# Attention scores from rounded high and low parts, with query heads paired by their key head's half of the rows

## What is computed

```python
def swiglu(h, wg, wu, wd):
    return (jax.nn.silu(h @ wg) * (h @ wu)) @ wd

def dense_block_attention(q, k, v, kc, vc):
    ...
    g = hq // hk
    qb = q.reshape(bsz, nb, GA_BLOCK, hk, g, d).transpose(1, 0, 2, 3, 4, 5)
    def one_block(qi):
        s_lat = jnp.einsum('bqhgd,bkhd->bhgqk', qi, k).astype(jnp.float32) * scale
        s_ctx = jnp.einsum('bqhgd,bkhd->bhgqk', qi, kc).astype(jnp.float32) * scale
        p_lat, p_ctx = joint_softmax([s_lat, s_ctx])
        return (jnp.einsum('bhgqk,bkhd->bqhgd', p_lat.astype(v.dtype), v)
                + jnp.einsum('bhgqk,bkhd->bqhgd', p_ctx.astype(vc.dtype), vc))
```

## Time and profile before

| | us |
|---|---|
| median of three runs | 2144.75 (2143.36 to 2147.09) |
| the profiled execution, its own time | 2144.07 |
| its span | 2142.3 |
| PE busy | 2104.7 (98%) |
| PEld busy | 1776.8 (83%) |
| DVE busy | 1390.7 (65%) |
| ACT busy | 1017.3 (47%) |
| POOL busy | 570.9 (27%) |
| granted TensorE clock, mean | 0.996 of full speed |

### The profile page before, as it was taken

The page is one execution under the profiler, slowest core; times in us unless marked ns, Lnnn a source line. Parts: engine busy times, 40 slices in busy tenths (PEclk is TensorE's granted clock), DMA queues, the critical chain, the costliest instruction groups (busy, mean ns, idle before and its releaser), DMA issues.

```text
span 2142.3 us, 31623 instructions
## 1 busy us (share of the span) xinstructions
PE 2104.7 (98%) x11813; PEld 1776.8 (83%) x11813; DVE 1390.7 (65%) x2104; ACT 1017.3 (47%) x1593; POOL 570.9 (27%) x615
## 2 busy tenths in 40 slices
PE   7999999999999999999999999999999999999998
PEld 4888888988766778988888898888889888898997
DVE  4767776865676456865665685545557869776555
ACT  4544545554555543553444453222345557645444
POOL 1556554402010036343343320000013201251000
PEclk9999999999999999999999999999999999999999
DMA  9577775723333354755555465545546455676664
GB/s 311 159 212 202 185 216 168 194 80 93 100 111 91 98 167 134 207 153 160 164 161 170 141 178 157 155 138 158 152 127 165 119 134 149 170 198 179 183 182 137
DMA packets 471963, 340.61 MB, mean 159 GB/s; under 512 B 13226, under 2 KB 437654, under 8 KB 471686
## 3 DMA queue, kind: packets, MB, share of 16 engines
q1 hardware_dynamic: 441312, 238.06, 38.8%
q0 software_dynamic: 29056, 96.35, 16.1%
q10 hardware_dynamic: 1446, 4.20, 0.5%
HBM read 326.98 MB, written 12.36 MB: 158 GB/s over the span
## 4 chain that ended last, share of the span: by engine, by line
PE 92%; DVE 4%; issue 2%; ACT 1%; DMA 1%; POOL 0%; SPq 0%; DVEq 0%; ACTq 0%; POOLq 0%
PE bank L837 20%; PE bank L838 20%; PE bank L842 20%; PE bank L905 4%; PE bank L915 4%; PE bank L906 4%; PE bank L989 2%; PE bank L990 2%; PE bank L995 2%; DVE w_lo L806 1%; PE bank L1347 1%; PE bank L1323 1%; PE bank L1333 1%; PE bank L1113 1%; PE bank L1112 1%
## 5 line engine op out<-in xcount | busy, mean ns | idle before, releaser
L806 DVE TENSOR_TENSOR w_lo<-raw,w_hi 128x1024 fp32r<-128x1024 f32 (+1 forms) x442 | 570.3, 1292 | 549.1 <-PE bank L842 336.5
L796 ACT ACTIVATE w_hi<-raw 128x1024 fp32r<-128x1024 f32 (+1 forms) x442 | 461.6, 1045 | 604.9 <-PE bank L838 288.1
L837 PE MATMUL bank<-h_hi,w_hi 128*128 128x512 f32 (+1 forms) x1728 | 597.3, 358 | 2.1 <-DVE X L2049 1.5
L838 PE MATMUL bank<-h_lo,w_hi 128*128 128x512 f32 (+1 forms) x1728 | 592.0, 355 | 0.0
L837 PEld LDWEIGHTS bank<-h_hi,w_hi 128*128 128x128 f32 x1728 | 326.5, 189 | 50.1 <-issue 1.9
L842 PE MATMUL bank<-h_hi,w_lo 128*128 128x512 f32 (+1 forms) x1728 | 367.1, 355 | 0.0
L838 PEld LDWEIGHTS bank<-h_lo,w_hi 128*128 128x128 f32 x1728 | 326.7, 189 | 46.4 <-issue 1.0
L842 PEld LDWEIGHTS bank<-h_hi,w_lo 128*128 128x128 f32 x1728 | 291.5, 189 | 45.5
L837 PE MATMUL bank<-inner_hi,w_hi 128*128 128x256 f32 (+1 forms) x654 | 204.2, 334 | 0.0
L838 PE MATMUL bank<-inner_lo,w_hi 128*128 128x256 f32 (+1 forms) x654 | 203.7, 333 | 0.0
L2485 POOL DMA_DIRECT2D wm<-in_w_mod_dram x128 | 92.6, 724 | 327.3 <-DVE bank L2020 274.9
(11 more groups left out here) (300 smaller groups left out, 3224.4 us busy)
## 6 DMA issues: line engine op xcount, KB each, us to landing
wm<-in_w_mod_dram POOLq DMA_DIRECT2D x128, 512.0 KB, 4.4
raw<-in_w_in_dram SPq DMA_DIRECT2D x108, 512.0 KB, 4.0
raw<-in_ffn_w_down_dram SPq DMA_DIRECT2D x94, 512.0 KB, 4.1
raw<-in_ffn_w_gate_dram SPq DMA_DIRECT2D x88, 512.0 KB, 4.5
raw<-in_ffn_w_up_dram SPq DMA_DIRECT2D x88, 512.0 KB, 3.9
raw<-in_w_out_dram SPq DMA_DIRECT2D x24, 512.0 KB, 4.0
raw<-in_ffn_w_down_dram SPq DMA_DIRECT2D x24, 384.0 KB, 4.0
raw<-in_w_branch_dram SPq DMA_DIRECT2D x16, 512.0 KB, 4.6
```

Source lines behind the costliest of these rows:

```text
L796: act.activation(w_hi[w_slot[n]][:, 0:unit.rows, :], raw[unit.slot][:, 0:unit.rows, :], ACT.Copy).then_inc(hi_made, 1)
L806: dve.tensor_tensor(w_lo[w_slot[n]][:, 0:unit.rows, :], raw[unit.slot][:, 0:unit.rows, :], w_hi[w_slot[n]][:, 0:unit.rows, :].bitcast(F32) ...
L837: pe.matmul(psum, w_hi[s][:, k, :], hi, start=(k == 0), stop=False)
L838: mm = pe.matmul(psum, w_hi[s][:, k, :], lo, start=False, stop=False)
```

## The change

Scores are computed in three passes of fp32r: q_hi by k_hi, q_lo by k_hi, q_hi by k_lo. Each pass issues the matmul of one row half and then of the other, so that the two banks' matmuls alternate. The parts come from here:

- `q_parts`, two buffers in turn: ACT rounds the task's 128 queries (`round_q`), DVE subtracts (`split_q`). Those of tasks 0 and 1 stand ahead of the turns, those of task t+2 at the end of turn t on DVE and after `exponents(t)` on ACT. `q_parts` lies in the place of `dt_t`, whose last reader is the DMA of the cumulative sums, so ACT first waits for that (`cum_stored`).
- Keys AK and CK get their parts by a new step "keys" at positions 12 and 13 of the projection, BK and BK+1 in turns 1 and 2 (`round_key` on ACT, `split_key` on DVE). `k_lo` is written over `K`; `k_hi_b` lies over the constants that only the projection reads. These are now a tile of their own, `cst_in`, which POOL's queue loads again for layer 1.

The query heads of A and C are loaded so that chunk i holds heads i and 2+i (`head_at`): each stands on the row half of its own key head. `k_swap`, its four DMAs and PE's waits for them are gone. In return a paired query chunk is loaded by two DMAs with runs of 64 floats, and a unit of branch weights by six DMAs, since the rows of the branch outputs stand in another order.

The tables, tiles, head order and loads:

```diff
+PAIRED = [AQ, AQ + 1, CQ, CQ + 1]
-        12: [("rope", 2), ("v", 0)], 13: [("rope", 3)], 14: [("conv", 5), ("dt", 0)], 15: [("rope", 4), ("v", 1)],
+        12: [("rope", 2), ("v", 0), ("keys", 0)], 13: [("rope", 3), ("keys", 1)], 14: [("conv", 5), ("dt", 0)], 15: [("rope", 4), ("v", 1)],
...
+            k_hi_b = sb("k_hi_b", [P, 2, TOK], F32R, scoring)
+        q_parts = sb("q_parts", [P, 2, 2, P], F32R)
-                k_swap = sb("k_swap", [P, 2, TOK], F32, mixer)
+                k_hi = sb("k_hi", [P, 2, TOK], F32R, mixer)
+                k_lo = sb("k_lo", [P, 14, TOK], F32R, scoring)
...
+        def head_at(br, i, hh):
+            return 2 * i + hh if br == 1 else 2 * hh + i
...
+            def paired_heads(l, col):
+                two = w_in[l].rearrange("(c p) n -> p c n", p=P)[:, :, col // (2 * P) * 2 * P:(col // (2 * P) + 1) * 2 * P]
+                heads = two.rearrange("p c (h i q) -> p c h i q", h=2, i=2)
+                return [(lambda t, h=h: t[:, :, h * HD:(h + 1) * HD], heads[:, :, h, col // P % 2, :]) for h in range(2)]
...
+                            for k in (1, 3):
+                                found.append(((2 * k, 2 * k + 2), w_branch[l, k].rearrange("(c p) n -> p c n", p=P)[:, :, d * P:(d + 1) * P]))
+                            for k in (0, 2):
+                                for h in range(2):
+                                    paired = w_branch[l, k].rearrange("(h c q) n -> h q c n", h=2, c=2)[h, :, :, d * P:(d + 1) * P]
```

PE, in `score(t)`, behind the waits for the exponents of task t-1:

```diff
-                        rows = slice(HD * hh, HD * hh + HD)
-                        q = chunk((AQ, BQ, CQ)[br] + i)[rows, st * LAT + qt * P:st * LAT + (qt + 1) * P]
...
-                            k = k_swap[:, br // 2]
-                        mm = pe.matmul(bank[hh][:, 0:TOK - keys.start], q, k[rows, keys], start=True, stop=True)
+                    q_split.wait(pe, (l, t))
+                    k_c = key_chunk(br, i)
+                    keys_split.wait(pe, (l, k_c))
+                    high, low = key_parts(k_c)
+                    for n_pass, (q_part, k) in enumerate(((0, high), (1, high), (0, low))):
+                        for hh in range(2):
+                            rows = slice(HD * hh, HD * hh + HD)
+                            mm = pe.matmul(bank[hh][:, 0:TOK - keys.start], q_parts[rows, t % 2, q_part, :], k[rows, keys],
+                                           start=(n_pass == 0), stop=(n_pass == 2))
```

ACT, at the start of the mixer and in its turns:

```diff
+                prep_done.wait(act, (l, "cumtok", 0))
+                cum_stored.wait(act, l)
+                for t in range(2):
+                    round_q(t)
                 for t in range(last_turn + 1):
...
                         exponents(t)
+                    if t + 2 < n_tasks:
+                        round_q(t + 2)
+                    if t in (1, 2):
+                        round_key(BK + t - 1)
```

DVE, the same:

```diff
+            def split_key(c, l):
+                keys_rounded.wait(dve, (l, c))
+                high, low = key_parts(c)
+                keys_split.done(dve.tensor_tensor(low, chunk(c)[:, :], high.bitcast(F32), ALU.subtract), (l, c))
...
+                for t in range(2):
+                    split_q(t)
                 for t in range(last_turn + 1):
...
                         normalise(t)
+                    if t + 2 < n_tasks:
+                        split_q(t + 2)
+                    if t in (1, 2):
+                        split_key(BK + t - 1, l)
```

POOL, the constants of layer 1's projection and the swapped keys:

```diff
+                    layer_loads.done(pool.dma_start(cst_in[:, :], consts[:, KEPT_CONSTS:CONSTS]))
-                for i in (1, 0):
-                    prepared.wait(pool, (l, "rope", ROTATED.index(SWAPPED[i])))
-                    for rows in range(2):
-                        swapped[i].done(pool.dma_start(k_swap[rows * HD:(rows + 1) * HD, i, :],
-                                                       chunk(SWAPPED[i])[(1 - rows) * HD:(2 - rows) * HD, :]), l)
```

More of the change, by code:

```diff
@@ L225, in plan_units @@
                 stage(("in", l), IN_CHUNKS, "product", DC)
+                for pos, c in enumerate(IN_ORDER):
+                    if c in PAIRED:
+                        units[first["in", l] + pos].dmas = 2
                 stage(("gates", l), EARLY, "product", DC)
@@ L229, in plan_units @@
                         stage(("gate", l, d + AHEAD), 1, "product", DC)
-                    stage(("branch", l, d), 1, "product", DC)
+                    stage(("branch", l, d), 1, "product", DC, 6)
                 stage(("out", l), sweep_steps(l, "out"), "product", DC)
@@ L315, in build @@
         smax = sb("smax", [P, 4, 4])
-        dt_t = sb("dt_t", [8, TOK])
+        with ExitStack() as projecting:
+            dt_t = sb("dt_t", [8, TOK], F32, projecting)
+        q_parts = sb("q_parts", [P, 2, 2, P], F32R)
         da_t = mod_row[0:8, :]
@@ L456, in build @@
         spread = signal("spread", 16)
-        swapped = [signal(f"swapped{i}", 16) for i in range(2)]
+        keys_rounded = signal("keys_rounded")
+        keys_split = signal("keys_split")
+        q_rounded = signal("q_rounded")
+        q_split = signal("q_split")
         gate_open = signal("gate_open")
@@ L712, in load @@
                         sp.wait_ge(lo_made, old.product - per[1] + 1 + i * per[1])
-                for rows, src in sources:
-                    sp.dma_start(raw[unit.slot][:, rows[0]:rows[1], :], src).then_inc(loaded[unit.slot], 16)
+                for place, src in sources:
+                    sp.dma_start(place(raw[unit.slot]) if callable(place) else raw[unit.slot][:, place[0]:place[1], :],
+                                 src).then_inc(loaded[unit.slot], 16)
             def stage(u0, n, source):
@@ L1376, in _ @@
                 projected.wait(pe, (l, IN_ORDER[-1]))
-                for i in range(2):
-                    swapped[i].wait(pe, l)
                 prepared.wait(pe, (l, "cumtok", 0))
@@ L1639, in prepare @@
                     prepared.wait(act, (l, "rope", 5))
-                    lo, hi = CONST_COLS["trif"][0], CONST_COLS["trib"][1]
-                    act_prepared.done(act.activation(tri_rows[:, 0:hi - lo], cst[:, lo:hi], ACT.Copy), (l, "tri"))
+                    lo, hi = CONST_COLS["trif"][0] - KEPT_CONSTS, CONST_COLS["trib"][1] - KEPT_CONSTS
+                    act_prepared.done(act.activation(tri_rows[:, 0:hi - lo], cst_in[:, lo:hi], ACT.Copy), (l, "tri"))
+                elif step == "keys":
+                    c = ROUNDED[i]
+                    prepared.wait(act, (l, "rope", ROTATED.index(c)))
+                    keys_rounded.done(act.activation(key_parts(c)[0], chunk(c)[:, :], ACT.Copy), (l, c))
                 elif step == "dt":
@@ L1795, in exponents, with round_q, round_key @@
                         exped.done(ins, (l, t, hh))
+                def round_q(t):
+                    br, i, st, qt = tasks[t]
+                    c = (AQ, BQ, CQ)[br] + i
+                    projected.wait(act, (l, c))
+                    q_rounded.done(act.activation(q_parts[:, t % 2, 0, :], chunk(c)[:, st * LAT + qt * P:st * LAT + (qt + 1) * P], ACT.Copy), (l, t))
+                def round_key(c):
+                    projected.wait(act, (l, c))
+                    keys_rounded.done(act.activation(key_parts(c)[0], chunk(c)[:, :], ACT.Copy), (l, c))
                 def decays(step, g, s):
@@ L2198, in prepare @@
                     prepared.done(dve.tensor_tensor(lat, lat, work, ALU.add), (l, "rope", i))
+                elif step == "keys":
+                    split_key(ROUNDED[i], l)
                 elif step == "v":
@@ L2301, in bound, with split_q @@
                         bounded.done(ins, (l, t, hh))
+                def split_q(t):
+                    br, i, st, qt = tasks[t]
+                    q_rounded.wait(dve, (l, t))
+                    q_split.done(dve.tensor_tensor(q_parts[:, t % 2, 1, :], chunk((AQ, BQ, CQ)[br] + i)[:, st * LAT + qt * P:st * LAT + (qt + 1) * P],
+                                                   q_parts[:, t % 2, 0, :].bitcast(F32), ALU.subtract), (l, t))
                 def normalise(t):
```

53 lines of the change are left out of this document (33 added, 20 removed).

## The result

The changed kernel takes 2149.47 us (median of 20 runs, 2146.27 to 2152.24), the kernel before 2144.53 us beside it (2142.39 to 2147.09). The ratio is 1.0023, with a 95% interval of 1.0017 to 1.0029: slower by a little over 0.2%. The time lies in the range of the prediction and 3.2 us above its forecast of 2146.3.

What follows compares the result with a forecast made beforehand. TensorE, with 92% of the span, was taken as the bound: 2144.07 - 4.7 (passes) + 4.4 (starts) - 0.1 and + 2.3 (turns) + 0.3 (projection) = 2146.3 us, range 2141 to 2151.5.

Steps and rivals of the forecast that it cites:

- The score passes: Score blocks of both layers: three rounded passes take 0.90 us (512 keys) and 0.57 us (256), -4.7 us in all.
- Rival A: Score blocks: row halves of rounded matmuls do not overlap, +16.2 us in place of -4.7, so 2167 us; chance 0.05.
- The starts: Start of each mixer: TensorE's first score waits for VectorE's query subtraction, +2.2 us a layer, +4.4 us in all.
- The clock: Behind the wait at each mixer start: the granted clock is not expected to answer, so no cost in the sum.
- Layer 1's projection: Layer 1's second key split stands before the conv and softplus chain TensorE waits for: +0.3 us, bounds 0 and 0.6.
- The turns: Mixer turns: added ScalarE and VectorE work delays TensorE, -0.1 us in layer 0, +2.3 us in layer 1 (bounds 0 and 4.5).
- The loads: Branch weights in six DMAs and paired query chunks in two: hidden, with 1.3 us to spare at worst.
- Rival B: Layer 1's mixer: VectorE becomes the bound and every stall goes on to the next, 2150.1 us; chance 0.15.

Runs made afterwards that it cites:

- both moves: Changed kernel with the query parts of tasks 0 and 1 and the parts of keys AK and CK at projection position 20: 2142.00 us, 0.9988 of before.
- the last kernel above: Kernel with both moves, minus VectorE's query subtractions and ScalarE's query roundings in the turns: 2141.58 us, 0.9981 of before.

## Why the prediction was right, and where it was wrong

The range held the time, and three of the steps held closely. The forecast missed it by 3.2 us, because a step that was set to nothing was not nothing. It would have missed by more if another term hadn't erred the other way, and that is luck: the clock, the projection and layer 0's turns cost 3.5 us more than the sum had, and layer 1's turns 1.8 us less.

- **The score passes.** 0.90 and 0.57 us were forecast for a block, 0.90 and 0.55 measured. The gain is 24 x 0.16 + 12 x 0.08 = 4.8 us for the 4.7 of the sum. The rate of the full-width rows was the right choice. The Trainium skill's page "FP8 and Floating Point Precision" (section TensorE Precision Notes) gives true FP32 four passes, and three of four would make 0.85 us by an estimate; the trace doesn't agree, it has 0.90. Rival A is out: the halves overlap in either order.
- **The starts.** 2.2 us a layer were forecast, 2.3 measured, released by the subtraction that was named.
- **The clock.** This is the step that failed: "The clock is not expected to answer", taken from the 1.63 us idle of the earlier trace rows with a clock of 1.00 around it. The wait of the sum was longer than the one in the row, 2.2 us against 1.63, so the row said nothing of it. And the same trace of the kernel before had a row against it. Two idle stretches of TensorE stand behind layer 1's attention, one of 1.90 us and, ahead of the second SwiGLU block, one of 2.78. The clock fell behind the shorter one and not behind the longer:

```profile
1910.55 0.36 PE L868 MATMUL bank<-h_hi,w_hi 128*128 128x256 f32 x1 [1.90 <-issue]
...
1943.78 0.36 PE L989 MATMUL bank<-h_hi,w_hi 128*128 128x256 f32 x1 [2.78 <-DVE h_lo L1949]
```

```profile
1911.00:1912.00 1.00, 1.00 (x9) 1.00 (x8) 0.93 (x3) 0.89 (x2) 0.47 (x2) 0.72 0.92 278
1912.00:1914.00 2.00, 2.00 (x11) 2.00 (x11) 1.47 (x3) 0.89 (x2) 0.34 (x1) 0.50 0.01 3
...
1944.00:1948.00 4.00, 3.55 (x29) 3.35 (x29) 3.79 (x8) 1.53 (x3) 0.00 (x0) 1.00 0.95 107
```

In the kernels of this study with the 2.3 us wait unfilled the clock fell behind 9 of 10 such starts, each time with some 1.7 us of clock; the one without is layer 0's in the kernel with plain passes. The kernel before with the wait alone shows it without anything else of the change, +7.1 us where the waits are 4.6. In the mean over the runs it is 2.5 us of clock that the sum lacked.
- **Layer 1's projection.** +0.3 us was forecast, within 0 to 0.6, and +0.9 measured. The term was mis-sized in its duration: the subtraction of a key chunk was taken at 0.6 us, from rows in which GpSimd computes nothing, and it stands beside GpSimd's bias work, where it takes 1.12. That it is these subtractions is shown by their move to position 20, which brings the wait back to 1.6 us. That the longer wait can bring down the clock too was not in the sum. It did so in three of the five kernels with a wait of 2.5 us there, and in two of the seven with 1.6.
- **The turns.** For layer 1 2.3 us were forecast. In the changed kernel the mixer is 0.4 us longer, with 1.8 us less of passes and 1.7 of clock, so about 0.5 us of added waits: the late and slowed TensorE hid them. Once it comes on time they are 2.9 us. The mechanism was right, and the place too (the gates of turns 1 and 2, the transposes of turn 3), but the engine was only half so: ScalarE's share is the larger. For layer 0 -0.1 was forecast. In the changed kernel its mixer is 0.8 us shorter, with 2.8 less of passes and 1.7 of clock, so about +0.3. With both moves it is 2.2 us shorter where the same passes (12 x 0.16 + 11 x 0.08) give 2.8, so it is +0.6, of which 0.5 is the gate of turn 1 (0.82 us for the 0.31 of before).
- **The loads.** Hidden, as forecast. No wait of TensorE ends on `raw` in the branch stage, and the six DMAs land in 2.7 and 2.9 us each in the median:

```profile
raw<-in_w_branch_dram SPq DMA_DIRECT2D x32, 128.0 KB, 2.7
raw<-in_w_branch_dram SPq DMA_DIRECT2D x64, 64.0 KB, 2.9
```

The sum with what was measured: 2144.5 - 4.8 + 4.6 + 0.9 + 0.3 + 0.5 + 2.5 = 2148.5 us, for 2149.5. The microsecond left lies within what the clock's term leaves open. That term is rough also because mean clock and time don't go together in every run: one of the last kernel above shows 0.980 at 2142.79 us. Rival B named 2150.1 us, the nearest figure, by a mechanism that is not the one: it wanted waits that carry on from turn to turn in layer 1. The prediction gave 0.71 to a time within 0.2% of before and 0.23 to a slower one, and the measured 1.0023 stands just over that bound, which its interval (1.0017 to 1.0029) reaches across.

## What to carry to other kernels

An instruction that a full engine waits for has to be placed by the queue that it stands in, not by its length: 0.28 us of subtraction cost 2.3 us of wait because two copies stood ahead of it, and moving it one position up, into 4 us of idle time, took the wait away. A new wait on TensorE should carry the price of a fall of the clock in the sum, at least as a bound, if it is as long as the shortest one behind which a trace of the kernel shows a fall. One wait without a fall is no argument, not even a longer one. The duration of an instruction is to be read from a row of the same place, beside the same work of the other engines. And when a stall is taken away, look first for what is late next: here about half of the gain of the shorter passes went to waits in the turns, most of them at the gates of layer 1, where the queues on ScalarE and VectorE had hardly any room for the work that the passes need.

## What was not expected of the hardware

- The granted clock went to 0.50 behind 2.3 us of idle time at a mixer's start in 9 of 10 cases, at v_tok behind 2.5 us in 3 of 5 and behind 1.6 us in 2 of 7, and behind the 2.8 us ahead of layer 1's second SwiGLU block in 6 of the 12 profiled executions. Each fall was for some 3.4 us, but for two of 6.8 at v_tok. So no length of idle time between 1.6 and 2.8 us parts the two outcomes here, and one execution with full clock behind 1.63 us doesn't say that the next one has it.
- A subtraction of 128 by 512 takes 0.68 us on VectorE while GpSimd computes nothing and 1.12 us beside GpSimd's work on the bias.
- Six matmuls over half the rows each, queued three and three, ran in pairs over both halves, the second half's first matmuls ahead of the first half's third: 0.90 us in this order as in the alternating one.
